# The start and the pace of a recurrence's softplus inside a one-core hybrid block

## The chip, the cores and the metric

One Trainium2 chip, one of its cores. The metric is the device time of one execution in microseconds (us). In the profile PE is TensorE (matmuls), ACT is ScalarE, DVE is VectorE, POOL is GpSimd and SP is SyncE, which issues the DMAs. The five engines run their own queues in order and meet by semaphores.

## The reference, cut to what matters

Three layers are computed for 512 tokens of width 1024. The first one mixes three branches: a gated MLP, an attention over compressed, selected and window keys, and a recurrence. The change is in the part where the recurrence and the compression lie side by side:

```
xc = conv4(xr) + conv_b
r = sigmoid(xh @ w_a + b_a);  i = sigmoid(xh @ w_x + b_x)
log_a = -8 * r * softplus(-lam)
a = exp(log_a);  b_in = sqrt(-expm1(2 * log_a)) * (i * xc)
h = scan(a, b_in);  y_c = h * gelu(gate)
compress(t) = gelu(blocks(t) @ w1) @ w2        # for keys and for values
```

`softplus(-lam)` depends on a parameter alone: 1024 numbers, a tile of 128x8.

## The kernel before, in words

Channels lie on partitions and tokens along the free axis, so a product is 8 tiles of 128x128 weights against 128x512 activations. All is float32 made of two rounded halves: ScalarE rounds a group of 8 weight tiles (`w_hi<-w_raw`, one 512 KB DMA), GpSimd makes the rest of it (`w_lo`), and TensorE does three matmuls for each tile (high by high, high by low, low by high). Five slots hold groups of weights; a slot is loaded again when TensorE is done with its group.

`walk` writes the order of all work. Every engine walks it and issues its own instructions, so an engine's queue has the walk's order. `run` advances a main piece, here a product, and calls `tick` after each tile. Side work is a generator handed to `later`; `yield n` in it means that it goes on n ticks later. A product is 8 ticks, a pair of gate products 2. When a side task is still open at `finish`, the rest of it is written at once.

In the stretch of the change the main pieces are eight products `conv` j, each followed by `evac_conv` (four VectorE instructions from the bank into `XC`, then ScalarE's `xs_hi<-XC` and VectorE's `xs_lo`), and behind product j the gate products of pair j-2 (`rnn_gates`), which read `xs` and end in two tanh on ScalarE (`TR`, `TI`). Beside them `compress` runs from product 0 on: hidden products for keys and values, a gelu behind each, and the small copies into `kc` and `vc`. Counted in ticks from product 0, its gelus come at ticks 24, 28, 41 and 45, and its last step at 53. Product 2 begins at tick 17, product 6 at tick 57 and product 7 at tick 67; the gates of pair 5 end at tick 76.

`softplus` is side work on VectorE and ScalarE: three VectorE steps on 128x8 (`soft_begin`), an exponential on ScalarE, a reciprocal with the addition before it, z and its square, the first value and eight pairs of multiply and add of a series (`soft_series`), and four last steps that write `coef` and `coefh`. `soft_recip` waits for the exponential. `soft_series(0)` has one step; every other has two, each waiting for the one before. At the end `finish(t_cmp)` and `finish(t_soft)` come, and `recurrence` starts: its VectorE step `TI<-TI,XC` and then exponential and tanh on ScalarE, scaled by `coef` and `coefh`. It goes on beside `groups(0)`: key product, gate pair 6, key product, gate pair 7, values, queries. The key products are evacuated by ScalarE (`keys_high`) and then VectorE (`keys_low`, `KS<-bank,KS`), and the bank is free after the second.

The main products take four banks in turn (6, 7, 0, 1); each waits until the bank's last evacuation has ended. A convolution's bank is free when VectorE's fourth instruction has ended, a gate product's when its tanh has.

ScalarE's functions need a table. A change of table shows as `ACT_TABLE_LOAD`.

Of the kernel before, what the change touches and what calls it, by code (L numbers as in the profile page):

```python
# [183 lines left out]
def program(nc, A, out):  # L184
# [204 lines left out]
    class Order:  # L389
# [332 lines left out]

        def softplus(self):
            self.soft_begin()
            yield 3
            self.soft_recip()
            yield 3
            self.soft_z()
            yield 3
            self.soft_series(0)  # L730
            for n in range(15, 0, -2):
                self.soft_series(n)
                yield 3
            self.soft_scale()
            yield 3
            self.soft_end()


# [646 lines left out]
        def walk(self):  # L1385
# [34 lines left out]

            self.gated = [False] * KT
            for j in range(KT):
                if j == 2:
                    t_soft = self.later(self.softplus())
                self.run(self.product(H, ("conv", j), self.evac_conv(j)))
                if j > 1:
                    self.run(self.rnn_gates(j - 2))
# [1678 lines left out]
```

## Time and profile before

| | |
|---|---|
| three runs, median (lowest to highest) | 2502.02 us (2501.56 to 3527.31) |
| profiled execution, its own time | 2501.5 us |
| its span, first to last instruction | 2499.6 us |
| granted TensorE clock, mean | 0.998 |
| PE, DVE, ACT, POOL busy | 99%, 46%, 42%, 45% |

All times of rows count from the span's start. In a timeline row the first number is the start, the second the length; "[... <-X]" is idle time ahead of it and what ended it.

### The profile page before, as it was taken

How to read it: one execution, taken by the hardware profiler on the slowest of the kernel's cores; microseconds unless marked ns; L12 is line 12 of the kernel's file. 1: busy time of each engine (PE TensorE's matmuls, PEld its weight loads, DVE VectorE, ACT ScalarE, POOL GpSimd, SP SyncE). 2: the span in 40 equal slices, each digit the busy share in tenths (PEclk: the TensorE clock that was granted, in tenths of full speed). 3: DMA queues.
4: the chain of work that ended last, by engine and by line, in shares of the span. 5: the costliest groups of instructions: out<-in, count | busy, mean ns of one | idle time of the engine just before them, and what ended most of it. 6: DMA issues, size and time to landing. Idle time of an engine off the chain costs nothing.

```text
span 2499.6 us, 33197 instructions
## 1 busy us (share of the span) xinstructions
PE 2484.2 (99%) x13326; PEld 2144.8 (86%) x13326; DVE 1140.4 (46%) x2332; ACT 1041.8 (42%) x2014; POOL 1132.2 (45%) x651
## 2 busy tenths in 40 slices
PE   9999999999999999999999999999999999999998
PEld 8888898888889888889888888888898888888888
DVE  7681487755415642325244455523234335444313
ACT  7553487742325332235343333333344333333323
POOL 3354455544445554444434445444543444444442
PEclk9999999999999999999999999999999999999999
DMA  5233322245332553332322222222322222222222
GB/s 213 76 102 105 98 78 73 64 166 196 128 133 77 202 192 111 105 103 71 105 84 77 85 81 93 80 91 95 110 92 83 78 85 88 82 87 82 93 100 77
DMA packets 89240, 258.86 MB, mean 104 GB/s; under 512 B 8960, under 2 KB 30208, under 8 KB 88704
## 3 DMA queue, kind: packets, MB, share of 16 engines
q1 hardware_dynamic: 89088, 256.74, 30.8%
q8 instruction: 106, 1.74, 0.3%
q14 instruction: 46, 0.38, 0.0%
HBM read 246.22 MB, written 2.10 MB: 99 GB/s over the span
## 4 chain that ended last, share of the span: by engine, by line
PE 91%; DVE 4%; ACT 3%; issue 1%; POOL 1%; DMA 0%; DVEq 0%; SPq 0%; POOLq 0%; ACTq 0%
PE bank L1809 88%; PE bank L1819 2%; ACT PP L2027 1%; DVE pt_lo L2328 0%; DVE Y L2328 0%; DVE nt L2328 0%; POOL n L2887 0%; ACT Hhi L2027 0%; DVE C L2328 0%; DVE PP L2587 0%; ACT pt_hi L2027 0%; ACT w_hi L2027 0%; ACT blkv L2027 0%; ACT blkk L2027 0%; DMA XR<-in_x 0%
## 5 line engine op out<-in xcount | busy, mean ns | idle before, releaser
L2882 POOL TENSOR_TENSOR w_lo<-w_raw,w_hi 128x1024 fp32r<-128x1024 f32 (+1 forms) x302 | 744.6, 2468 | 851.0 <-ACT w_hi L2027 850.9
L1809 PE MATMUL bank<-Hhi,w_hi 128*128 128x512 f32 (+1 forms) x1700 | 657.3, 387 | 0.0
L1809 PE MATMUL bank<-Hhi,w_lo 128*128 128x512 f32 (+1 forms) x1700 | 651.4, 383 | 0.0
L1809 PE MATMUL bank<-Hlo,w_hi 128*128 128x512 f32 (+1 forms) x1700 | 651.3, 383 | 0.1
L2027 ACT ACTIVATE w_hi<-w_raw 128x1024 fp32r<-128x1024 f32 (+1 forms) x318 | 325.9, 1029 | 117.3 <-DMA w_raw<-in_wa 84.0
L1809 PEld LDWEIGHTS bank<-Hhi,w_lo 128*128 128x128 f32 x1700 | 320.1, 188 | 63.8
L1809 PEld LDWEIGHTS bank<-Hlo,w_hi 128*128 128x128 f32 x1700 | 320.6, 189 | 57.4 <-POOL w_lo L2882 0.5
L1809 PEld LDWEIGHTS bank<-Hhi,w_hi 128*128 128x128 f32 x1700 | 320.5, 189 | 56.8
L2882 POOL TENSOR_TENSOR w_fifth_lo<-w_fifth_raw,w_fifth_hi 128x1024 fp32r<-128x1024 f32 x77 | 191.7, 2489 | 230.5 <-ACT w_fifth_hi L2027 230.5
L1809 PE MATMUL bank<-Hhi,w_fifth_hi 128*128 128x512 f32 x404 | 161.2, 399 | 0.0
L1809 PE MATMUL bank<-Hhi,w_fifth_lo 128*128 128x512 f32 x404 | 157.6, 390 | 0.0
L1809 PE MATMUL bank<-Hlo,w_fifth_hi 128*128 128x512 f32 x404 | 157.6, 390 | 0.0
L2907 POOL TENSOR_SCALAR PP<-PP,small 128x128 f32<-128x128 f32 (+3 forms) x128 | 66.1, 538 | 73.2 <-DVE small L2328 72.8
L1809 PE MATMUL bank<-Y,w_hi 128*128 128x512 f32 x304 | 93.6, 389 | 0.0
L2027 ACT ACTIVATE w_fifth_hi<-w_fifth_raw 128x1024 fp32r<-128x1024 f32 x77 | 81.5, 1058 | 24.1 <-DMA w_fifth_raw<-in_wa 20.1
L1809 PEld LDWEIGHTS bank<-Hhi,w_fifth_lo 128*128 128x128 f32 x404 | 75.8, 188 | 16.5
L1809 PE MATMUL bank<-w_hi,Hhi 128*128 128x256 f32 (+2 forms) x296 | 89.6, 303 | 0.0
L1809 PE MATMUL bank<-w_lo,Hhi 128*128 128x256 f32 (+2 forms) x296 | 89.3, 302 | 0.0
L1809 PE MATMUL bank<-w_hi,Hlo 128*128 128x256 f32 (+2 forms) x296 | 89.2, 301 | 0.0
L1809 PEld LDWEIGHTS bank<-Hhi,w_fifth_hi 128*128 128x128 f32 x404 | 76.0, 188 | 13.2 <-issue 0.2
L1809 PEld LDWEIGHTS bank<-Hlo,w_fifth_hi 128*128 128x128 f32 x404 | 76.1, 188 | 12.9
L2617 DVE CUSTOM_DVE_ANT_0 wm<-wm,c 128x1024 f32<-128x1024 f32 x48 | 79.7, 1664 | 7.1 <-DMA wm<-in_w_ada 6.8
(415 smaller groups left out, 4819.1 us busy)
## 6 DMA issues: line engine op xcount, KB each, us to landing
w_raw<-in_wb SPq DMA_DIRECT2D x169, 512.0 KB, 3.4
w_raw<-in_wa SPq DMA_DIRECT2D x139, 512.0 KB, 3.4
wm<-in_w_ada SPq DMA_DIRECT2D x48, 512.0 KB, 4.4
w_fifth_raw<-in_wb SPq DMA_DIRECT2D x42, 512.0 KB, 3.5
w_fifth_raw<-in_wa SPq DMA_DIRECT2D x35, 512.0 KB, 3.4
QQ<-Y SPq DMA_DIRECT2D x64, 128.0 KB, 2.4
wa_raw<-in_wb SPq DMA_DIRECT2D x5, 512.0 KB, 6.4
XR<-in_x SPq DMA_DIRECT2D x4, 512.0 KB, 7.1
```

The lines of the kernel that those rows point to most:

```text
L1809: return self.e.matmul(o, lhs, rhs, start=start, stop=stop)
L1819: return self.e.transpose(o, i, ident[0:n, 0:n])
L2027: return self.e.activation(o, a, func, **kw)
L2617: self.e.tensor_tensor_reduce(x, x, cc[l][:, :], .5, 0., ALU.mult, ALU.add, mod[:, l, n:n + 1]).then_inc(*dve_mod("row", l, n))
L2882: self.e.tensor_tensor(x.lo[:, k:k + n, :], x.raw[:, k:k + n, :], f(x.hi[:, k:k + n, :]), ALU.subtract).then_inc(*w_rest(s, k))
L2907: self.e.tensor_scalar(p, p, r[:, n:n + 1], 1., ALU.mult, ALU.mult).then_inc(*pool_nsa("p", u, n))
```

## The change

`softplus` is handed to `later` before product 6 and not before product 2, and its steps come two ticks apart and not three. With that `soft_begin` falls on tick 57 (before: 17), the reciprocal on 58 (19), z on 60 (22), the first value and the first pair on 62 (25), the other pairs on 64, 66, 68, 70, 72, 74 and 76 (28, 31, 34, 37, 40, 43, 46), and the four last steps are written by `finish`, just ahead of the recurrence (before: ticks 49 and 52). The same instructions are issued; only their places in the queues of VectorE and ScalarE differ.

```diff
--- before.py
+++ after.py
@@ -722,17 +722,17 @@
 
         def softplus(self):
             self.soft_begin()
-            yield 3
+            yield 2
             self.soft_recip()
-            yield 3
+            yield 2
             self.soft_z()
-            yield 3
+            yield 2
             self.soft_series(0)
             for n in range(15, 0, -2):
                 self.soft_series(n)
-                yield 3
+                yield 2
             self.soft_scale()
-            yield 3
+            yield 2
             self.soft_end()
 
 
@@ -1420,7 +1420,7 @@
 
             self.gated = [False] * KT
             for j in range(KT):
-                if j == 2:
+                if j == 6:
                     t_soft = self.later(self.softplus())
                 self.run(self.product(H, ("conv", j), self.evac_conv(j)))
                 if j > 1:
```

## Rows read from the trace of the kernel before

**Rows 1.** The page, part 1: busy time of each engine.
```profile
PE 2484.2 (99%) x13326; PEld 2144.8 (86%) x13326; DVE 1140.4 (46%) x2332; ACT 1041.8 (42%) x2014; POOL 1132.2 (45%) x651
```

**Rows 2.** Waits of PE, 36 to 260 us: total, times, longest.
```profile
PE bank L1809 <- ACT TR L2027: 1.6, 1, 1.6
```

**Rows 3.** Timeline, DVE, 38 to 112 us: start, length, instruction, idle before.
```profile
57.59 2.37 DVE L2332 TENSOR_SCALAR tiny<-tiny 128x8 f32<-128x8 f32 x1
...
60.97 0.81 DVE L2333 TENSOR_SCALAR XC<-bank,par 128x512 f32<-128x512 f32 x1
...
72.78 2.36 DVE L2332 TENSOR_SCALAR tiny<-tiny 128x8 f32<-128x8 f32 x1
...
76.56 0.18 DVE L2328 TENSOR_TENSOR kc<-bank,kc 64x32 fp32r<-64x32 f32 x1
```

**Rows 4.** Timeline, POOL, 38 to 165 us.
```profile
57.57 2.37 POOL L2882 TENSOR_TENSOR w_lo<-w_raw,w_hi 128x1024 fp32r<-128x1024 f32 x1 [2.71 <-ACT w_hi L2027]
...
99.66 2.40 POOL L2882 TENSOR_TENSOR w_lo<-w_raw,w_hi 128x1024 fp32r<-128x1024 f32 x1 [8.36 <-ACT w_hi L2027]
102.97 4.78 POOL L2882 TENSOR_TENSOR w_lo<-w_raw,w_hi 128x1024 fp32r<-128x1024 f32 x2 [0.90 <-ACT w_hi L2027]
```

**Rows 5.** Timeline, ACT, 38 to 110 us.
```profile
57.51 1.28 ACT L2027 ACT_TABLE_LOAD   x1
60.00 0.21 ACT L2027 ACTIVATE tiny<-tiny 128x8 f32<-128x8 f32 x1 [1.20 <-DVE tiny L2332]
...
67.22 0.68 ACT L2027 ACTIVATE TR<-bank,half 128x512 f32<-128x512 f32 x1
```

**Rows 6.** Timeline, PE, 60 to 82 us.
```profile
66.02 0.39 PE L1809 MATMUL bank<-xs_hi,w_fifth_lo 128*128 128x512 f32 x1
67.96 0.50 PE L1809 MATMUL bank<-xs_hi,w_fifth_hi 128*128 128x512 f32 x1 [1.55 <-ACT TR L2027]
...
76.32 0.39 PE L1809 MATMUL bank<-Hhi,w_lo 128*128 128x512 f32 x1
76.80 3.84 PE L1809 MATMUL bank<-blkv,w1v 128*128 128x128 f32 x32
```

**Rows 7.** Timeline, ACT, 98 to 160 us.
```profile
98.53 1.06 ACT L2027 ACTIVATE w_hi<-w_raw 128x1024 fp32r<-128x1024 f32 x1
101.31 0.63 ACT L2027 ACTIVATE xs_hi<-XC 128x512 fp32r<-128x512 f32 x1 [1.73 <-DVE XC L2336]
...
102.80 0.67 ACT L2027 ACTIVATE TR<-bank,half 128x512 f32<-128x512 f32 x1
...
109.57 1.28 ACT L2027 ACT_TABLE_LOAD   x1
110.87 0.81 ACT L2027 ACTIVATE XC<-TR,coef 128x512 f32<-128x512 f32 x1
```

**Rows 8.** Timeline, DVE, 98 to 130 us.
```profile
98.12 0.81 DVE L2333 TENSOR_SCALAR XC<-bank,par 128x512 f32<-128x512 f32 x1
...
104.57 0.81 DVE L2333 TENSOR_SCALAR XC<-bank,par 128x512 f32<-128x512 f32 x1 [1.90 <-PE bank L1809]
...
109.04 1.89 DVE L2336 SCALAR_TENSOR_TENSOR TI<-TI,XC 128x512 f32<-128x512 f32 x3
...
116.54 1.41 DVE L2328 TENSOR_TENSOR KS<-bank,KS 64x512 fp32r<-64x512 f32 x2
```

**Rows 9.** Timeline, PE, 103.5 to 130 us.
```profile
104.37 0.39 PE L1809 MATMUL bank<-xs_hi,w_fifth_hi 128*128 128x512 f32 x1
...
118.00 0.50 PE L1809 MATMUL bank<-xs_hi,w_hi 128*128 128x512 f32 x1
```

**Rows 10.** Timeline, DVE beside three POOL instructions, 1806 to 1812 us.
```profile
1807.61 1.67 DVE L2328 TENSOR_TENSOR nB<-nB,nB 128x256 f32<-128x256 f32 x1 [0.48 <-ACT nB L2027]
...
1806.39 7.66 POOL L2882 TENSOR_TENSOR wa_lo<-wa_raw,wa_hi 128x1024 fp32r<-128x1024 f32 x3
```

**Rows 11.** Stretches: length, busy time, then PEclk, DMA share, GB/s.
```profile
1165.00:1170.00 5.00, 5.00 (x31) 5.00 (x32) 3.72 (x12) 2.70 (x9) 0.00 (x0) 0.67 0.00 0
```

## The prediction

> **What bounds the kernel now.** I began with the busy shares: TensorE is busy for 2484.2 of 2499.6 us [rows 1], so only a wait of TensorE that goes, or one that comes, can move the end. Next I read the waits of TensorE from 36 to 260 us, the stretch in which softplus, compression, convolution and recurrence run. There is one, 1.6 us, for ScalarE's TR [rows 2]. Then I read that stretch engine by engine as a timeline, to see what stands ahead of that TR and how near the other releases are.
>
> The chain behind the wait: VectorE's third small step took 2.37 us, where the small copy at 76.56 takes 0.18 [rows 3], since GpSimd had begun a w_lo 0.02 us before [rows 4]. ScalarE had loaded a table meanwhile and could run the exponential only at 60.00 [rows 5]. VectorE stood still for it, and the convolution of product 2 began at 60.97 [rows 3]. xs_hi and the first TR (67.22) follow on ScalarE [rows 5], and this TR frees the bank of the gate product that started at 67.96 [rows 6].
>
> **Banks.** The main banks go round in fours, so a product waits for the evacuation of the one four places before it. Call the gate products of pair j Gj0 and Gj1. Then G11 waits for the tanh of G00; G50 for convolution 6 on VectorE; G51 for the tanh of G40; G60 for convolution 7; G61 for the tanh of G50; G70 for VectorE's second half of the first key product.
>
> **What is removed.** Without softplus at this place convolution 2 starts behind xs_lo at 57.2, not at 60.97 [rows 3], and everything behind it on ScalarE comes 3.8 us sooner: TR at 63.4, over by 64.1. G11 could start at 66.02+0.23 = 66.25; it started at 67.96 [rows 6]. So 1.71 us go, and 0.11 more, since the first product after the wait is 0.50 long and not 0.39. A second, smaller one: the values' hidden product started at 76.80, 0.48 behind the product before it where 0.23 is the pace [rows 6], when the last kc copy ended [rows 3]; the kc copies stood behind a small step that took 2.36 us [rows 3]. That goes too: 0.25+0.11. Sum 2.18 us, and TensorE, VectorE and ScalarE come to the seventh product 2.17 us sooner. I take both whole: behind the first there are 2 us of room, behind the second 2.6.
>
> One table load goes (gelu's own stays, since tanh and gelu run on one table, and exponential and tanh of the recurrence on another): the one at 109.57 [rows 7] moves to the new place. Alone it is worth nothing to TensorE, unless ScalarE is late there.
>
> **What is added, in order.** The times are the present ones less 2.17.
>
> (a) xs_lo of product 5 leaves VectorE at 98.12-2.17 = 95.95; today convolution 6 begins right there [rows 8]. Now softplus's first three steps come (0.6 us) and then the wait for ScalarE. The queue there: w_hi from 98.53-2.17 = 96.36 to 97.42 (1.06), table load 1.28, exponential 0.21 [rows 5, 7]: done at 98.96. What is queued behind this wait on VectorE is convolution 6.
>
> (b) That w_hi starts a w_lo on GpSimd at 99.66-2.17 = 97.49, for 2.40 us [rows 4]. The step behind the exponential reads and writes SBUF alone; such a step, met by a running w_lo, ended with it, at 57.59 and at 72.78 [rows 3]. So it ends at 99.9. This lock is also what the Trainium skill says (SBUF — State Buffer, "Who interferes with whom"): of a VectorE and a GpSimd instruction on the shared ports the one that started first keeps them for its whole length.
>
> (c) Six more small steps at 0.2 us (inverse, z, its square, the first series value, one series pair): convolution 6 begins at 101.1, 3.0 later than today and 5.15 late against TensorE.
>
> (d) Its evacuation takes 3.15 (98.12 until just ahead of xs_hi at 101.31 [rows 7, 8]), so until 104.25. Without waits G50 would start at 104.37-2.17 = 102.20 [rows 9]. New wait 2.05, and 0.11. Then xs_hi at 104.3, a w_hi, and the tanh of G40 at 101.31 to 102.80 behind it [rows 7], so from 105.8 to 106.45. G51 is due at 105.1: wait 1.4 and 0.11. The first key product starts at 107.3 and not at 105.73 (two gates of 0.68 behind 104.37): the gain of 2.17 is spent, and 1.6 more.
>
> (e) Behind xs_lo of product 6, 4.47 after its convolution (104.57 to 109.04, [rows 8]), five series pairs stand before convolution 7: ten steps, 2.05 us, from 105.6. The two w_lo that run back to back from 102.97 for 4.78 us [rows 4] now come at 105.95 and 108.4. A waiting step with two SBUF inputs gets in between two of them: one that started at 1807.61, inside three in a row, lasted 1.67 us [rows 10]. So one step passes at 108.4, the next at 110.8, and the other six or so in 1.2: convolution 7 begins at 112.0, evacuated at 115.15. G60 is due at 107.3+24x0.227 = 112.75: wait 2.4 and 0.11. G61 waits for the tanh of G50 (until 116.4): 0.4 and 0.11. The second key product starts at 117.25.
>
> (f) xs_lo of product 7 and eight last steps (1.5) bring coefh to 117.9 and the recurrence's first VectorE step to 117.85 to 118.5. ScalarE, which needs both, starts its first exponential at 118.5 and not at 110.87 [rows 7], 7.66 later, the saved table load already counted. From there to the key product's second half, which today ends at 116.54+1.41 = 117.95 [rows 8], the two engines go hand in hand with hardly a gap, so that half ends at 125.6. G70 started at 118.00, right on that release [rows 9]; now at 125.65. It is due at 117.25+5.45 = 122.7, so a wait of 3.0.
>
> **The sum.** G70 is 7.65 us late, and so are VectorE and ScalarE behind it. From there to 306 us TensorE has no wait, and later ones hang on chains that shift with it, so nothing is given back. Counted on TensorE: -2.18 + 2.16 + 1.51 + 2.5 + 0.5 + 3.1 = 7.6. The profiled execution took 2501.5 us (span 2499.6): 2501.5+7.7 = 2509.2 us, 0.3% slower. The three runs' median is 0.5 above the profiled one, which is inside what the forecast can tell. A measurement of this kernel tells 2% from no change, so the verdict is "same" in all cases here. The queues of GpSimd and SyncE hold the same instructions in the same order, no DMA is moved past another, and weights are asked for when TensorE is done with a group, so they shift with it; the w_hi at 98.53 waited for no landing [rows 7]. DMA therefore counts as nothing.
>
> The unknown is how the small steps pass the w_lo's in (b) and (e). Bounds: with no blocking in (e), convolution 7 begins at 107.6, the recurrence 4.4 sooner (first exponential at 114.1, key halves done at 121.2), and the sum is +3.3. With one of the two blocks it is +5.5. If the blocks are each a little longer (the 1.67 of [rows 10] was 0.4 of work and 1.3 of wait, ending 0.3 after the boundary) +8.5. I take 7.7, by the steps of 2.37 and 2.36, which are of the same kind and size.
>
> A place where the skill would give another sum: ScalarE: Activation LUTs, "What ACT_TABLE_LOAD costs", has 1.28 us for the load and 1.38 more for a drain. The row at 109.57 shows 1.28 and the next instruction at 110.87. By the page, called an estimate, the exponential of (a) would end at 100.3, convolution 6 would start 0.4 later and the sum would be 8.1.
>
> **Rivals.** *The gain comes free* (faster side): -2.2 us, 2499.3. Its condition is that convolution 6 is evacuated before G50 is due; today it has 104.37-101.27 = 3.1 us of room, and it would have to be late by less. For it: the old wait is real and surely goes. Against it: w_hi, table load and exponential alone hold VectorE from 96.5 to 98.96, and seven steps follow: 4.2 without any lock. The rule of the same page of the skill to group by table (section "Table sets") speaks for this case, as there is one load fewer.
>
> *Waits that cost only once*: +3.3 us, 2504.8, the bound above: the small steps slip between the w_lo's, or G70's release turns out to have slack in ScalarE's queue.
>
> *TensorE's clock falls*: the waits add up to 9.3 us between 102 and 126. From 1165 to 1170 the granted clock was 0.67 of full, after waits shorter than these [rows 11]; that is 1.65 us lost, 1.0 being 2.4 GHz. At 68 us, after a wait of 1.55, it did not fall. One such fall gives 2510.9, two 2512.5.
>
> *The change does nothing that counts*: G70 is held by something else than the chain of (f), and the two ends cancel: 2501.5, between the first two.
>
> **Chances.** Forecast (2506.5 to 2510) 0.5; clock falls (2510 to 2513) 0.15; costs only once (2503 to 2506.5) 0.15; nothing 0.05; gain free 0.15. All are within 2%; by the forecast 50 us would be needed to leave it. The range from 2499.0 to 2513.0 takes in the free gain, without which 0.15 and more would be left out at one end together with what is above 2513. Faster by over 2%: 0.01, within: 0.98, slower: 0.01. The likeliest case's own range is 2506.5 to 2510.
>
> **What the profile after would show.** Right: no exponential of 128x8 near 60; G11 on pace at 66.25; a table load near 97.4 and none near 109; a small step of about 0.9 us at 99; convolution 6 at 101; TensorE's waits at 102, 105, 113 and 123 for VectorE's XC, ScalarE's TR, XC and KS; two small steps over 2 us between 105 and 111; the recurrence's first exponential near 118.5. Wrong: no new waits of TensorE up to 130, or waits of which the one before G70 is missing. It would be wrong as well if later chains, above all those of the 300 to 520 stretch, took up or lost some us.

## The result, and the profile after

The changed kernel takes 2509.11 us (median; 2508.29 to 2512.18) where the kernel before takes 2502.02 on the same chip: ratio 1.0032, 95% interval [1.0023, 1.0041], so slower by 5.7 to 10.3 us and within 2%. One execution of the kernel before took 3527.31 us and isn't used in the ratio. 2509.2 was predicted. The profiled execution took 2508.74 us, with a span of 2506.9.

The page's busy times of the changed kernel:

```profile
PE 2485.5 (99%) x13326; PEld 2144.9 (86%) x13326; DVE 1139.2 (45%) x2332; ACT 1040.3 (41%) x2013; POOL 1131.3 (45%) x651
```

TensorE's busy time rose by 1.3 us against [rows 1], its span by 7.3: most of the time is in waits. ScalarE's one instruction fewer is the table load that goes. The waits between 36 and 300 us (total, times, longest):

```profile
PE bank L1809 <- DVE KS L2328: 2.8, 1, 2.8
PE bank L1809 <- DVE XC L2336: 2.4, 2, 1.9
PE bank L1809 <- ACT TR L2027: 1.5, 2, 1.2
```

The one wait of [rows 2] is gone and five others are there. The timeline of TensorE shows each, at G50, G51, G60, G61 and G70:

```profile
105.31 0.50 PE L1809 MATMUL bank<-xs_hi,w_fifth_hi 128*128 128x512 f32 x1 [1.92 <-DVE XC L2336]
107.49 0.63 PE L1809 MATMUL bank<-xs_hi,w_fifth_hi 128*128 128x512 f32 x1 [1.21 <-ACT TR L2027]
116.01 0.50 PE L1809 MATMUL bank<-xs_hi,w_hi 128*128 128x512 f32 x1 [0.47 <-DVE XC L2336]
117.25 0.50 PE L1809 MATMUL bank<-xs_hi,w_hi 128*128 128x512 f32 x1 [0.27 <-ACT TR L2027]
126.47 0.50 PE L1809 MATMUL bank<-xs_hi,w_hi 128*128 128x512 f32 x1 [2.81 <-DVE KS L2328]
```

What holds those banks is on the other three engines. ScalarE's table load and small exponential, its first gate tanh behind convolution 6, and the recurrence's first exponential (these answer to [rows 5, 7]):

```profile
98.45 1.28 ACT L2027 ACT_TABLE_LOAD   x1
99.75 0.21 ACT L2027 ACTIVATE tiny<-tiny 128x8 f32<-128x8 f32 x1
...
106.77 0.67 ACT L2027 ACTIVATE TR<-bank,half 128x512 f32<-128x512 f32 x1
...
119.35 0.82 ACT L2027 ACTIVATE XC<-TR,coef 128x512 f32<-128x512 f32 x1 [1.58 <-DVE TI L2336]
```

VectorE (to [rows 3, 8]): the step behind the exponential, convolution 6, the two long small steps, convolution 7, and the halves of the first key product:

```profile
99.99 0.94 DVE L2332 TENSOR_SCALAR tiny<-tiny 128x8 f32<-128x8 f32 x1 [2.44 <-ACT tiny L2027]
...
102.10 0.81 DVE L2333 TENSOR_SCALAR XC<-bank,par 128x512 f32<-128x512 f32 x1
...
106.96 2.38 DVE L2328 TENSOR_TENSOR tiny<-tiny 128x8 f32<-128x8 f32 x1
109.37 2.30 DVE L2332 TENSOR_SCALAR tiny<-tiny 128x8 f32<-128x8 f32 x1
...
112.80 0.81 DVE L2333 TENSOR_SCALAR XC<-bank,par 128x512 f32<-128x512 f32 x1
...
125.01 1.41 DVE L2328 TENSOR_TENSOR KS<-bank,KS 64x512 fp32r<-64x512 f32 x2
```

And GpSimd's weight remainders beside them (to [rows 4]):

```profile
98.51 2.39 POOL L2882 TENSOR_TENSOR w_lo<-w_raw,w_hi 128x1024 fp32r<-128x1024 f32 x1 [8.35 <-ACT w_hi L2027]
106.94 4.70 POOL L2882 TENSOR_TENSOR w_lo<-w_raw,w_hi 128x1024 fp32r<-128x1024 f32 x2 [6.03 <-ACT w_hi L2027]
```

The step at 99.99 ends at 100.93, 0.03 behind the `w_lo` that began at 98.51. The step at 106.96 begins 0.02 behind the next `w_lo` and ends at 109.34, near the seam of the two; the one at 109.37 ends at 111.67, with the second.

**One more thing has to be read before times are subtracted.** The whole stretch lies 1.07 us later in this execution, for something far ahead of the change, in the first 9 us. It isn't the granted clock, although that was 0.91 in the changed kernel's first 20 us: it read 1.00 until 8 us, when TensorE was already late, and the kernel e3 (below) is 1.10 us later with a clock of 1.00 throughout. In the twelve profiled executions this offset lies between -0.31 and +1.10 us. Part of it shows as TensorE's wait for ScalarE's `Ghi` near 8 us, 0.5 us before, 1.8 after and 1.2 in e3; what makes it vary stays open. Windows (length, busy times, then PEclk, DMA share, GB/s) of the changed kernel, and the first one of e3:

```profile
0.00:20.00 20.00, 17.06 (x112) 16.69 (x113) 12.54 (x32) 14.41 (x35) 0.20 (x4) 0.91 0.70 236
1165.00:1170.00 5.00, 5.00 (x44) 5.00 (x43) 4.90 (x8) 2.41 (x7) 2.94 (x3) 1.00 0.00 0
...
0.00:20.00 20.00, 17.29 (x112) 16.52 (x113) 12.54 (x32) 14.40 (x35) 0.20 (x4) 1.00 0.70 236
```

So I count each kernel from its own first hidden product (the first matmul that reads `blkk`): 48.87 us before, 49.94 after. G70 starts 69.13 us behind it before [rows 9] and 76.53 after: +7.40, where the prediction has +7.65. The span's 7.3 is this 7.4, 1.07 more from the start, and 1.2 back later: 1.5 at 1165 to 1170, where the clock had fallen to 0.67 before [rows 11] and stayed at 1.00 here, and 0.3 lost again behind it.

### The profile page after: what moved, and what is told of

It is laid out like the page before. It is cut to its first block, busy times and chain, and to the rows that moved or that the text cites. A ratio compares the mean times of both kernels' runs of the same rounds, so it can differ in the third digit from the quotient of the medians.

```text
span 2506.9 us, 33196 instructions
## 1 busy us (share of the span) xinstructions
PE 2485.5 (99%) x13326; PEld 2144.9 (86%) x13326; DVE 1139.2 (45%) x2332; ACT 1040.3 (41%) x2013; POOL 1131.3 (45%) x651
## 4 chain that ended last, share of the span: by engine, by line
PE 92%; DVE 4%; ACT 2%; POOL 1%; issue 1%; DMA 0%; SPq 0%; DVEq 0%; POOLq 0%; ACTq 0%
PE bank L1809 89%; PE bank L1819 2%; ACT PP L2027 1%; DVE pt_lo L2328 0%; DVE Y L2328 0%; POOL n L2887 0%; DVE C L2328 0%; DVE PP L2587 0%; ACT pt_hi L2027 0%; DVE XC L2336 0%; DVE nt L2328 0%; DMA XR<-in_x 0%; DMA wf_raw<-in_wa 0%; ACT w_hi L2027 0%; ACT Hhi L2027 0%
```

## The experiments

Ten kernels, each made from one of the two. "G70" is G70's start behind the first hidden product, against before's 69.13; the time is the median against that of the kernel before in the same series of runs (2502.0 us for the change, 2501.1 for e1 to e4, 2500.9 for e5, e6, e8 and e9, 2501.4 for e7 and e12). The code cuts of e3, e4, e5, e8 and e12 are against the changed kernel, that of e1 against the kernel before.

| kernel | G70 | time | ratio, 95% interval |
|---|---|---|---|
| the change | +7.40 | +7.1 | 1.0032 [1.0023, 1.0041] |
| e1 place only | +7.36 | +8.7 | 1.0033 [1.0020, 1.0045] |
| e2 pace only | +1.86 | +1.3 | 1.0006 [0.9996, 1.0015] |
| e3 exponential ahead | +4.01 | +4.1 | 1.0016 [1.0007, 1.0026] |
| e4 series behind | +4.31 | +4.2 | 1.0016 [1.0007, 1.0026] |
| e7 both of them | +0.96 | +0.9 | 1.0005 [0.9996, 1.0014] |
| e12 series in PSUM | +3.96 | +3.9 | 1.0014 [1.0005, 1.0024] |
| e8 six banks up to the keys | +13.01 | +12.7 | 1.0049 [1.0035, 1.0063] |
| e9 six banks through the keys | +4.19 | +6.0 | 1.0021 [1.0012, 1.0030] |
| e5 all of it before product 4 | -2.22 | -2.5 | 0.9989 [0.9980, 0.9998] |
| e6 no softplus | -2.19 | -2.35 | 0.9989 [0.9981, 0.9998] |

### Which half of the change costs

**e1**, the place alone:

```diff
-                if j == 2:
+                if j == 6:
                     t_soft = self.later(self.softplus())
```

> Softplus at product 6 as in the change, but its steps three ticks apart as before. Theory (the small steps on VectorE are one queue ahead of the recurrence, whatever their spacing; what counts is their number and the two w_lo they run into): convolution 7 starts about 1.2 us sooner than in the change (7 small steps ahead of it, not 10), so TensorE's wait for it shrinks by 1.2, and the 14 steps behind it end when the 8 end now; the wait for KS grows by what the other lost. G70 comes 7.4 us later than before, as in the change (7.39), +7.3 in time within 0.5. Rival (the pace decides): with the old pace at least 2 us of the loss go, +5 or less.

**e2**, the pace alone: each `yield 3` of `softplus` becomes `yield 2`, and `j == 2` stays.

> Softplus at product 2 as before, its steps two ticks apart. Theory: three more small steps stand ahead of convolution 2, 0.6 us, so TensorE's wait for TR grows from 1.6 to about 2.2; in return the steps are over before the kc copies, and the 0.35 us at the values' hidden product goes. Sum +0.3 us for G70, same time within 0.5. No waits behind 80 us. Rival (the pace alone makes new waits): a wait of TensorE for XC or KS between 100 and 126 us, over 1 us.

e1 has the whole +7.36, so the place is the cause. Six of the small steps that the change has ahead of convolutions 6 and 7 stand behind 7 here, so that one starts 1.2 us nearer and its waits are cut otherwise; but G70, behind all of them, is where the change has it. The time, +8.7, missed the expected 7.3 within 0.5. In this profile the clock fell once more during G70's wait of 3.99 us (0.50 from 125 to 129), and the matmul at 130.70 is 9.6 us late where the change is 7.4. The two ratios, 1.0033 and 1.0032, don't tell the kernels apart.

e2 missed its expectation, +1.86 where +0.3 stood. The old wait at G11 grew, and something came behind it. TensorE's rows:

```profile
69.29 0.50 PE L1809 MATMUL bank<-xs_hi,w_fifth_hi 128*128 128x512 f32 x1 [2.15 <-ACT TR L2027]
...
70.77 0.80 PE L1809 MATMUL bank<-Hhi,w_fifth_hi 128*128 128x512 f32 x1
```

and the windows behind them:

```profile
70.00:72.00 2.00, 2.00 (x9) 1.45 (x8) 1.76 (x3) 1.07 (x2) 2.00 (x2) 0.70 0.00 0
72.00:74.00 2.00, 2.00 (x10) 1.90 (x10) 1.47 (x2) 2.00 (x4) 1.44 (x1) 0.50 0.00 0
```

and the first of them in the kernel before:

```profile
70.00:72.00 2.00, 2.00 (x18) 1.96 (x17) 1.42 (x1) 2.00 (x4) 2.00 (x1) 1.00 0.00 0
```

The wait is 2.15 us, 0.60 longer than before's 1.55 [rows 6], and the granted clock went to 0.50, which is 1.2 GHz, until about 74. Behind before's wait the clock stayed at 1.00. By the windows the loss is 2 x 0.30 + 2 x 0.50 + 0.1 = 1.7 us at the most. Matmul by matmul it is 1.55: just ahead of the values' hidden product the kernel is 2.15 us late. There 0.27 comes back (0.35 had been expected), which leaves the +1.86 of G70. So the theory's two terms came as expected, and what it lacked is the fall of the clock.

### The two prices of the change

**e3** puts the first three steps, the exponential and the addition and reciprocal behind it ahead of convolution 5's copies; the rest stays where the change has it.

```diff
+            yield 4
             self.soft_begin()
-            yield 2
+            yield 8
             self.soft_recip()
...
-                if j == 6:
+                if j == 5:
```

> The change, but its first step and the exponential come at tick 50 (behind the w_hi that ScalarE rounds in product 5, where ScalarE and VectorE are idle); all other steps at the ticks of the change. Theory: VectorE no longer stands still for ScalarE, convolution 6 starts 3.7 us sooner, TensorE's waits of 1.9 for XC and 1.2 for TR go; the two w_lo still block two small steps ahead of convolution 7, so the wait for it comes back in full (2 to 2.4 us) and the one for KS stays at 2.5 to 3.5. G70 +3.9 against before, time +3.9 (3 to 5). Rival (the wait for the exponential is not what delays, the lock and the number of steps are): G70 +6.5 or more.

**e4** keeps the change's start and puts the series from 13 down behind convolution 7.

```diff
             self.soft_series(0)
-            for n in range(15, 0, -2):
+            self.soft_series(15)
+            yield 12
+            for n in range(13, 0, -2):
                 self.soft_series(n)
-                yield 2
             self.soft_scale()
-            yield 2
             self.soft_end()
```

> The change, but the series pairs from 13 down come behind convolution 7 and not ahead of it; as many small steps stand ahead of the recurrence, ScalarE's and GpSimd's queues are the same. Theory with the lock: convolution 7 starts right behind xs_lo of product 6, no small step meets the first of the two w_lo, xs_lo of product 7 meets the second and ends 1.2 late. TensorE's wait for convolution 7 is gone, the one for KS stays near 3; G70 +4.8 against before, 2.6 less than the change. Rival (no lock, only the number of steps counts): G70 +7.4 as in the change.

**e7** does both.

> Both halves of the cure at once, with the placement at the seventh product kept: the first three steps and the exponential stand four ticks earlier than convolution 5's end, as in the kernel with the exponential ahead, and the series from 13 down stands behind convolution 7, as in the kernel with the series behind. My theory (two separate prices: 3.4 us of G70's delay for VectorE's wait for the exponential ahead of convolution 6, and 3.1 for the series steps and their two blocks ahead of convolution 7): they add up, G70 comes 7.4 - 3.4 - 3.1 = 0.9 us later than in before, time +1 (0 to +2). Rival (the two share one price, since either one alone makes the other wait harmless or worse): as the better of the two, +4.

e3 gives +4.01, so what it moves from ahead of convolution 6 is worth 3.4 us at G70: VectorE's wait of 2.44 for w_hi, table load and exponential, the step of 0.94 held by a `w_lo`, and four short ones. The single shares weren't tested. In its profile the clock fell at the end of G70's wait of 2.82, and 1.5 us more are lost behind G70; this execution took 2507.0 us, the longest of its ten, and the median is +4.1.

e4 gives +4.31, so taking the steps from ahead of convolution 7 is worth 3.1. The steps themselves are not saved, since they still stand ahead of the recurrence. What goes is the two blocks, 4.3 us beyond the steps' own work, and what comes is one of 1.1, as expected: `xs_lo` of product 7 is now the instruction that meets a `w_lo`, and takes 1.80 instead of 0.69.

```profile
110.07 1.80 DVE L2328 TENSOR_TENSOR xs_lo<-XC,xs_hi 128x512 fp32r<-128x512 f32 x1 [0.70 <-ACT xs_hi L2027]
...
106.60 4.72 POOL L2882 TENSOR_TENSOR w_lo<-w_raw,w_hi 128x1024 fp32r<-128x1024 f32 x2 [6.04 <-ACT w_hi L2027]
```

If the two prices are separate, e7 has to show 7.4 - 3.4 - 3.1 = +0.9, and it shows +0.96. Its waits, 36 to 300 us:

```profile
PE bank L1810 <- DVE KS L2329: 2.3, 1, 2.3
PE bank L1810 <- ACT TR L2028: 0.3, 1, 0.3
PE bank L1810 <- issue: 0.2, 1, 0.2
```

The waits at G50 and G60 are gone. The two small ones are at G40 and G41, since the steps moved ahead of convolution 5 start it 0.8 us later; they give back 0.9 of the 2.2 that were removed. G70's 2.3 us is the rest: 18 small steps still stand between `xs_lo` of product 7 and the recurrence.

e4 had been expected at +4.8, with a wait of near 3 at G70. There is none, since TensorE's clock was at 0.50 from about 106 to 113 and G70 came only at 123.04, when the key half had ended at 122.99. The slow clock cost nothing there: it took the wait's place.

### Is it the lock, or just the steps?

**e12** is the change with the series' value, `c[5]`, in a PSUM bank that is free in this stretch. The ten steps keep their places, but now each touches PSUM.

```diff
         def soft_series(self, n):
-            c = [tiny[:, 8 * i:8 * i + 8] for i in range(8)]
+            c = [tiny[:, 8 * i:8 * i + 8] for i in range(5)] + [banks[5][:, 0:8], tiny[:, 48:56]]
```

(the same line in `soft_scale`)

> The change, with the one intermediate value of the series (c[5], 128x8) in a PSUM bank that is free in this stretch, so that each step of the series and the log step read or write PSUM; the steps, their number and their places in the queues are the change's. My theory (the two steps of 2.38 and 2.30 us before convolution 7 are small steps held by GpSimd's w_lo on a port of SBUF, and the lock takes only steps with both operands in SBUF): the ten steps take 2 to 2.5 us, convolution 7 begins 4 us sooner than in the change, at about 59 us after the first hidden product instead of 62.9, and G70 is about 3.3 late instead of 7.4; the step behind the exponential stays blocked as before, and G50's and G51's waits stay. Time +3 to +5 over before. Rival (the time is that of the semaphores and of VectorE's queue, whatever memory the operand lies in, or a step with one SBUF operand is held all the same): two steps of 2.3 us are there again and the time is the change's, +7.5.

VectorE's timeline, steps three and four of the ten, which were the long ones, and convolution 7:

```profile
105.59 0.17 DVE L2328 TENSOR_TENSOR bank<-bank,tiny 128x8 f32<-128x8 f32 x1
105.80 0.17 DVE L2332 TENSOR_SCALAR bank<-bank 128x8 f32<-128x8 f32 x1
...
107.13 0.80 DVE L2333 TENSOR_SCALAR XC<-bank,par 128x512 f32<-128x512 f32 x1
```

with GpSimd at its two `w_lo` all the while:

```profile
105.56 4.72 POOL L2882 TENSOR_TENSOR w_lo<-w_raw,w_hi 128x1024 fp32r<-128x1024 f32 x2 [6.04 <-ACT w_hi L2027]
```

Each step takes 0.17 us right inside the `w_lo`. Convolution 7 begins 58.6 us behind the first hidden product (48.56 in this kernel) where it was 62.9, and the recurrence's first exponential at 65.1 and not 69.4. So the 4.3 us are the lock and not the steps, and the rival is out. The rule of the Trainium skill (SBUF — State Buffer, "Who interferes with whom") is borne out on both sides by these rows: a VectorE instruction with two SBUF inputs, or a `tensor_scalar` from SBUF to SBUF, can meet GpSimd's port; with at most one SBUF input and outside such a mode it doesn't.

G70 is at +3.96, where the release is at 72.23 (the key half ends at 120.79) against 69.08: +3.15. The other 0.8 is the clock. It fell behind the waits at G50 and G51:

```profile
105.00:107.00 2.00, 0.93 (x3) 0.80 (x3) 1.73 (x10) 2.00 (x4) 1.44 (x1) 0.50 0.02 4
107.00:109.00 2.00, 2.00 (x6) 1.52 (x6) 1.90 (x5) 0.58 (x1) 2.00 (x2) 0.50 0.04 8
109.00:111.00 2.00, 2.00 (x7) 1.52 (x6) 1.27 (x3) 0.68 (x2) 1.27 (x1) 0.50 0.00 0
```

### Are banks a way out?

**e8** is the change with six main banks in turn for convolutions and gates, and four again when the recurrence starts.

```diff
-            self.main.which, self.wide.which = [6, 7, 0, 1], list(range(8))
+            self.main.which, self.wide.which = [6, 7, 0, 1, 4, 5], list(range(8))
...
             t_rnn = self.later(self.recurrence())
+            self.main.which = [6, 7, 0, 1]
```

> The change as it is, with six PSUM banks in turn for the convolutions and gates instead of four, and four again from the keys' products on. My theory (each wait of TensorE at G50 and G51 is one for a bank that comes back late; but the steps themselves stay late, and the recurrence's start with them): the waits of 1.92 + 0.11 and 1.21 + 0.11 us at G50 and G51 go, as do those at G60 and G61, but the last half of the keys' evacuation still ends as late as in the change, so that the wait at G70 grows to 5 to 7 us and G70 and the time stay within 1 us of the change, +6 to +8 over before. Rival (the waits add up one by one, each is a price by itself): the four waits' 3.9 us are saved, time +3 to +4.

**e9** goes back to four only behind the first group's key products.

> The change with six PSUM banks in turn from the convolutions until the last of the keys' products. My theory: a product then waits for the copy of two banks earlier, so the waits at G50, G51, G60 and G61 go and the one at G70 becomes shorter, since only one wait of some 4 to 5 us for a bank is left among the keys' products; G70 2.5 us later than in before, time +2.5 to +5. Rival (VectorE's and ScalarE's work behind convolution 7 is itself the bound, not the number of banks): +7 as the change.

e8 is worse than both theories had it, by a fault of my edit. Its first key product:

```profile
116.15 0.79 PE L1810 MATMUL bank<-Hhi,w_fifth_hi 128*128 128x512 f32 x1 [12.63 <-ACT TR L2028]
```

It waits for the tanh that ran from 115.42 to 116.09, that of G50, two products earlier. Shortening the list moved the place in the turn onto a bank just used. It tells nothing of the two theories, but shows that G50 and G51 ran without a wait (at 102.00 and 102.67), and what one bank in the wrong place costs: the wait, and 2.6 us of slow clock behind it.

e9 is the clean one. Its waits are these:

```profile
104.07 0.50 PE L1811 MATMUL bank<-Hhi,w_fifth_hi 128*128 128x512 f32 x1 [0.75 <-DVE XC L2338]
...
114.83 0.50 PE L1811 MATMUL bank<-Hhi,w_hi 128*128 128x512 f32 x1 [3.67 <-DVE XC L2338]
...
125.31 0.41 PE L1811 MATMUL bank<-w_hi,Hhi 128*128 128x304 f32 x1 [0.95 <-DVE KS L2330]
```

The gates' waits are gone; one for convolution 6's bank and one for convolution 7's stand in their place, 4.4 us together, where one of 4 to 5 was expected. Behind the longer one some of the matmuls ran 0.43 apart and not 0.23, and G70 came 1.6 us later for that (114.83 + 0.11 + 5.45 = 120.39 was due, 122.02 is measured): hence +4.2 and not +2.6. Then the next wait for `KS` took another 0.95. The recurrence's first exponential is at 118.17 here, 69.5 behind the first hidden product, as in the change (69.4; before, 62.0). So both theories have a part: more banks let TensorE run on, but VectorE and ScalarE stay 7.5 late, and TensorE meets that again. The time, +6.0, is past the expected range, and its interval overlaps that of the change. In the traces e9 is 5.3 us late behind its last wait where the change is 7.4.

### What the softplus costs at best

**e5** writes the whole softplus at once in front of product 4, where both engines wait for TensorE:

```diff
             for j in range(KT):
-                if j == 6:
-                    t_soft = self.later(self.softplus())
+                if j == 4:
+                    t_soft = None
+                    for _ in self.softplus():
+                        pass
                 self.run(self.product(H, ("conv", j), self.evac_conv(j)))
...
-            self.finish(t_soft)
```

> The whole softplus in one piece in front of convolution product 4 (tick 37), where the trace of before has ScalarE and VectorE waiting for TensorE's products; none of it is left behind the compression's gelus or between the convolutions. My theory (the softplus costs only what its steps make a bank come back late, and TensorE's two waits of before, 1.71 + 0.11 and 0.25 + 0.11 us, are its whole price there): both waits go and none comes in their place, G70 starts 2.2 us earlier after the first hidden product than in before, and the time is 2.2 us under before, ratio 0.9991. Rival (a small step is never free: some 20 steps and an own table load of ScalarE in one piece hold back a copy of convolution 4): a wait of 1 to 3 us at convolution 4's or 5's gates, time between before and +1. Rival (the time lies elsewhere and the waits of this stretch do not reach the end): no difference from before.

**e6** leaves the softplus out and makes `coef` and `coefh` of the parameter itself, so it computes another recurrence; it is a bound only.

> The softplus is left out: the two coefficients are made of the input lambda itself, so the kernel computes another recurrence. It is the bound of what any place for the softplus can give. My theory: G70 starts 2.2 us earlier after the first hidden product than in before, time -2.2 us, the same as for the softplus in front of product 4 within 0.5 us. If the softplus costs something wherever it stands, this kernel is under that one by 1 us or more.

e5 has no wait of TensorE from 36 to 300 us. VectorE's row of convolution 4, behind all small steps, and ScalarE's load and exponential at the new place:

```profile
81.40 0.81 DVE L2334 TENSOR_SCALAR XC<-bank,par 128x512 f32<-128x512 f32 x1 [0.61 <-PE bank L1810]
```

```profile
71.62 1.28 ACT L2028 ACT_TABLE_LOAD   x1
73.42 0.21 ACT L2028 ACTIVATE tiny<-tiny 128x8 f32<-128x8 f32 x1 [0.52 <-DVE tiny L2333]
```

VectorE is done with `coefh` at 80.80 and still waits 0.61 for the product. One of the steps was held there too, for 2.33 us at 74.72 by a `w_lo` begun at 74.66, and ScalarE makes 34 table loads, where the change makes 32 and the kernel before 33; neither costs anything, since the room is 9 us (e6's VectorE waits 8.62 at this place). G70 comes at -2.22, e6's at -2.19, and the times agree within 0.2 us: in this place the softplus is free. e5 is the version that beats both kernels: the one before by 2.5 us (0.5 to 5.0 by the interval), the changed one by 9.6, which adds two separate comparisons.

## Why the prediction was right

Right in the sum and nearly right in its steps. That 2509.2 and 2509.11 differ by only 0.1 us is luck: the rise was put at 7.7 us on 2501.5, and it was 7.1 on 2502.0, with an interval of 5.7 to 10.3. The sharper test is G70, +7.65 predicted and +7.40 measured. Times after are less 1.07, to stand beside the prediction's.

| step | predicted | measured |
|---|---|---|
| what is removed | -2.18 | -2.19 (e6) |
| (a) exponential done | 98.96 | 98.89 |
| (b) small step ends with `w_lo` | 99.9 | 99.86 |
| (c) convolution 6 | 101.1 | 101.03 |
| (d) waits G50, G51 | 2.05, 1.4 | 1.92, 1.21 |
| (e) convolution 7 | 112.0 | 111.73 |
| (e) waits G60, G61 | 2.4, 0.4 | 0.47, 0.27 |
| (f) first exponential | 118.5 | 118.28 |
| (f) key half ends; wait G70 | 125.6; 3.0 | 125.35; 2.81 |

**The locks** of (b) and (e) were the unknown, and the value taken holds: both steps of (e) were held, for 2.38 and 2.30 us, the second one between the two `w_lo`. The lower bound, no block in (e), is e12's measurement: the key half +3.15 where the prediction had +3.3.

**The one term mis-sized** is the wait at G60, 2.4 predicted and 0.47 measured. The clock rival came true at this very place. Windows of the changed kernel:

```profile
107.00:109.00 2.00, 1.51 (x4) 1.23 (x5) 2.00 (x1) 1.96 (x3) 2.00 (x1) 0.68 0.01 4
109.00:111.00 2.00, 2.00 (x6) 1.54 (x6) 1.97 (x2) 0.00 (x0) 2.00 (x2) 0.50 0.04 8
```

Eight matmuls ran 0.43 us apart, 1.6 us more in all, and TensorE came that much later to a bank that wasn't free yet. The other 0.3 is from convolution 7, which was itself 0.27 sooner. The prediction had added such a fall to the sum (2510.9); it is hidden, because G60's release is VectorE's and in this trace came after TensorE all the same. In e1 and e3 the clock fell at G70 (in e1 for the second time), where nothing late follows to hide it, and the traces show 2.2 and 1.5 us lost there. So the rival's condition came true and its price depended on the place.

**The gain comes free** fails on convolution 6: 5.1 us late against 3.1 of room, as the prediction said. **Waits that cost only once** fails on the locks; e12 is that case. **Nothing counts** fails on e6 and e5, where taking the waits away shows in the time.

**Nothing given back** holds from G70 to 1160 us. There the two profiles draw 1.5 us nearer by the clock fall of [rows 11], which only one of them has. Of the twelve profiled executions four show a fall between 1165 and 1175 (before, e4, e9, e12) and eight don't, with no order by how late they are; what decides it stays open.

The load took 1.28 us and the exponential began 0.02 behind it. By the Trainium skill (ScalarE: Activation LUTs, "What ACT_TABLE_LOAD costs") a switch has 1.38 us of drain on top; the trace shows none on either side of the load, since the `w_hi` ahead of it ended 0.02 before it. So the sum without it was the better one.

## What to carry to other kernels

Here side work on a helper engine cost what it made a bank come back late, and at times a fall of the clock behind such a wait. Look for a place where that engine waits for the bottleneck (here 9 us before convolution 4) and put all of it there in one piece, even at the price of one more table load, before thinning it out over a stretch in which the engines go hand in hand. A step that has to wait for another engine must not stand ahead of an evacuation: moved earlier, the exponential with the steps around it gave back 3.4 us. When small SBUF steps lie beside GpSimd's long ones, count the lock (here 2.3 us for a step of 0.17) and not the steps, or give each step an operand in PSUM if a bank is free.

## What the runs showed that I had not expected

- **The clock fell behind some waits and not behind others, and their length doesn't tell which.** After 1.55 us [rows 6], 1.62 (e3 at G60) and 2.27 (e7) it stayed at 1.00. After 2.15 us (e2), after two waits of 1.07 to 1.93 with three matmuls between (the change, e1, e4, e12), and at 3.67 (e9), 3.99 (e1) and 12.63 (e8) it went to 0.50, for 3.4 or 6.8 us and in e8 for 13.7, with 512-column matmuls 0.43 apart where 0.23 is the pace. At G70 the change's 2.81 left it at 1.00 from 125 to 131, and e3's 2.82 took it down. What decides it stays open.

```profile
123.11 0.80 PE L1810 MATMUL bank<-xs_hi,w_hi 128*128 128x512 f32 x1 [2.82 <-DVE KS L2329]
...
123.00:125.00 2.00, 1.89 (x5) 1.51 (x6) 1.35 (x3) 1.97 (x4) 0.81 (x1) 0.51 0.00 0
```

- **Whether a fall costs depends on what is late next.** 1.6 us were lost in the change under G60's wait, 2.8 in e4 under what would have been G70's, and 2.6 in e12, of which 0.8 show at G70. At G70 in e1 and e3, and in e9, it stands in full.
- **More banks turn the waits around instead of removing them.** With six, the change's five waits, 6.7 us, become three (0.75, 3.67 and 0.95), and the clock fell behind the longest.
- **A PSUM operand is enough.** A 128x8 `tensor_tensor` with one input in PSUM and the other in SBUF takes 0.17 us inside a `w_lo`, as does the `tensor_scalar` from PSUM to PSUM.
